# Moving the normalisation of the linear heads one slot earlier in a hybrid decoder block

## The chip, the cores and the metric

The kernel runs on one core of one Trainium2 chip. Its time is the device time in microseconds of one launch. The engines are TensorE (PE, with its weight loads as PEld), VectorE (DVE), ScalarE (ACT), GpSimd (POOL) and SyncE (SP, which here issues nearly all transfers).

## What is computed

A decoder block: a combined input projection of the normalised input, four linear-recurrence heads and eight attention heads over a window of 128 tokens, an output projection, a gated feed-forward network and a last normalisation. The change touches what follows the recurrence of the linear heads, and the norm of the next tokens' input:

```python
def rmsnorm(x, g):
    xf = x.astype(jnp.float32)
    y = xf * lax.rsqrt(jnp.mean(xf * xf, axis=-1, keepdims=True) + EPS)
    return (y * g.astype(jnp.float32)).astype(x.dtype)
...
    o = o_intra + jnp.einsum('bhnck,bhnkv->bhncv', q_dec, s_prev)
    o = o.transpose(0, 2, 3, 1, 4).reshape(bsz, s, A_HEADS, A_DV)
    o = o * lax.rsqrt(jnp.mean(o * o, axis=-1, keepdims=True) + EPS)
    o = o.reshape(bsz, s, A_WIDTH) * norm_g.astype(f32) * jax.nn.silu(g.astype(f32))
...
        u = rmsnorm(h, ln1_g[l])
        proj = u @ w_in[l]
```

There are 2048 tokens, the model is 1024 wide, a linear head has 128 keys and 128 values, and everything is float32.

## The kernel before

The tokens come in four blocks of 512 (`it`, 0 to 3). Every engine has its own program, written out by hand, and waits for the others at semaphores. For each block the mixers run in 27 **slots** (0 to 26), then `out_b` does the last four columns of the output projection. After the four blocks come the feed-forward products, in two pairs of blocks. A product of float32 operands is made of three matmuls of split halves (lines 850 to 852): high by high, low by high, high by low. The halves of a weight tile are made by ACT (`make_hi`, L1217) and DVE (`make_lo`, L1685).

In slots 0 to 21 PE first does one group of 24 such matmuls (a column of the input projection), then small pieces of the mixers. In slots 22 to 26 the groups are those of the output projection by `A_PLAN`: input parts 0 and 1 in slot 22, 2 in slot 23, 4 and 5 in slot 24, 6 in slot 25, 7 and 3 in slot 26; part 3 is the last linear head.

The linear head `a` begins in slot `F_SLOT[a]` (4, 9, 14, 18), and its steps have offsets from there. Before the change the output is made at offset 5 (slots 9, 14, 19, 23), the root and the factor at 6 (slots 10, 15, 20, 24), the turn and the gate at 7 (slots 11, 16, 21, 25). The steps of one head, in order:

- PE `output` (L1015, L1021), and ACT squares and sums it per token block (L1277, `output`), both in the slot of OUTPUT.
- ACT `head_sum` takes the root (L1283, `hnrm`). Root on the one side, and exponential and tanh on the other, need different function tables in ACT, so a table load stands before each change of kind. DVE `head_sum` takes the reciprocal (L1814) and multiplies (L1816, `sqo`). In head 0 the root of the block before for the second norm goes with it (L1358, L1998). These are the steps of NORM_SUM.
- PE `head_turn` transposes `sqo` (L1029) after the group of its slot; DVE `head_mul` multiplies by the gate (L1827); ACT splits off the high half (L1289), DVE `head_lo` the low half (L1832). These are the steps of NORM_MUL.

In the slot loop of DVE `head_sum` stands near the end and `head_mul` near the start, ahead of `make_lo`:

```python
                    mul = head_at(slot, NORM_MUL)
                    if mul is not None:
                        head_mul(it, mul)
                    n = unit_made_at(slot)
                    if n is not None:
                        wait_unit_used(dve, it, n)
                        make_lo(it, n)
```

Around these steps, at the end of a block:

- Slot 21 has the sum of the attention squares on PE (L866), which waits for POOL's addition (L2321, semaphore `s_oacc`); POOL gets to it after the keys of head 3 (L2271, L2274), which wait for DVE's second reciprocal of slot 20 (L1774).
- Slot 21 also has PE's turn of head 3's values (L978) and ACT's copy of it (`iv`, L1262). PE waits for that copy at `key_turn` (L999) in slot 22, after 12 matmuls.
- Slots 19 to 26 have `x_turn` (L1041 on PE, L1328 on ACT): eight transposes that bring the input tokens into the bank that the residual is made from. The first four read first halves, the last four, in slots 23 to 26, second halves, into the same buffers `xs`. SP issues the second halves (L573) in `mixers`, in its one queue: behind the weights of unit 25 the first, of unit 26 the second, of unit 27 the third, of unit 28 the fourth. The weights of unit 27 (L562) wait until DVE has made the low half of unit 25, since both use one buffer. In the last block all four second halves are issued ahead of unit 26.
- ACT makes the sums of squares of the next block's first two token blocks (`stats`, L1224) and their root (`roots`, L1230) in slot 21, DVE scales by them in slot 24 (L1698). In the last block the first splits of the feed-forward operands (L1503 on ACT, L2013 on DVE) stand there, and their loads (L632) in SP's queue behind those of units 26 to 28.

Of the kernel before, what the change touches and what calls it, by code (L numbers as in the profile page):

```python
# [67 lines left out]
BV_TURN = 3  # L68
SWA_SUM, SWA_MUL = 21, 22

KEY_PRODUCTS, V_TURN, KEYS, UPDATE, OUTPUT, NORM_SUM, NORM_MUL = 2, 3, 3, 4, 5, 6, 7

H_TURN, H_STORE, H_SPREAD, H_SCALE = 2, 6, 11, 12
X_LOAD, X_STATS, X_SCALE = 12, 21, 24
# [22 lines left out]
def unit_made_at(slot):  # L97

    return {23: None, 24: 25, 25: 26, 26: None}.get(slot, slot + 2)
# [14 lines left out]
def head_part(slot):  # L114

    for a, first in enumerate(F_SLOT):
        if 0 <= slot - first < 4:
            return a, slot - first
    return None, None


def head_at(slot, offset):

    return F_SLOT.index(slot - offset) if slot - offset in F_SLOT else None
# [7 lines left out]
def block_program(nc, x, ln1_g, w_in, lb_logits, hgrn_norm_g, attn_sinks, attn_norm_g, w_out, ln2_g,  # L132
# [3 lines left out]
    NSB = S // T  # L136
# [33 lines left out]
    with ExitStack() as ctx:  # L170
# [90 lines left out]
        def tile(name, k, shape=(P, T), dt=F32):  # L261
            return at(name, shape, mix_at + 2 * K * k, dt)
# [8 lines left out]
        pr_dump = tile("pr_dump", 12, (P, D))  # L271
# [12 lines left out]
        x_next = [os_[0], os_[1], xs[0], xs[1]]  # L284
# [230 lines left out]
        def wait_unit_used(eng, it, n):  # L515

            eng.wait_ge(s_group, it * UNITS + n - 1)
# [690 lines left out]
        def _(act):  # L1208
# [4 lines left out]
            def make_hi(it, n):  # L1213

                s, k = n % 2, it * UH + n // 2
                act.wait_ge(s_raw[s], k * 16 + 16)
                A(whi[s][:, :, :], raw[s][:, :, :], ACT.Copy).then_inc(s_hi[s], 1)  # L1217


            def stats(it, b, src, dump):  # L1220
                act.wait_ge(s_x0[b], it * 16 + 16)
                if b:
                    act.wait_ge(s_xss, it * TB + b)
                A(dump[:, :], src[:, :], ACT.Square, accum_out=xss[:, b:b + 1]).then_inc(s_xss, 1)  # L1224

            def roots(it, b0, b1):
                act.wait_ge(s_xss, it * TB + b1)
                if it:
                    act.wait_ge(s_xn, it * TB)
                A(xnrm[:, b0:b1], xss[:, b0:b1], ACT.Sqrt, scale=1.0 / D, bias=epst[:, 0:1]).then_inc(s_xroot, 1)  # L1230
# [9 lines left out]
            def head_group(it, a, part, bank):  # L1240
                if part == 0:
                    if a:
                        act.wait_ge(s_ktr, it * HEADS + a)
                    A(forget[:, :], bank, ACT.Tanh, scale=0.5).then_inc(s_tf, 1)
                if part == 1:
                    if a:
                        act.wait_ge(s_qdec, it * HEADS + a)
                    A(gateq[:, :], bank, ACT.Tanh, scale=0.5).then_inc(s_tq, 1)
                if part == 2:
                    if a:  # L1250
                        act.wait_ge(s_ivtr, it * HEADS + a)
                    A(ivT[:, :], bank, ACT.Copy).then_inc(s_iv, 1)
                if part == 3:
                    if a >= 2:
                        act.wait_ge(s_yalo, it * HEADS + a - 1)
                    A(gate[a % 2][:, :], bank, ACT.Tanh, scale=0.5).then_inc(s_tg, 1)
# [7 lines left out]
            def key_turn(it, a):  # L1264
                act.wait_ge(s_ktr, it * HEADS + a + 1)
                if a:
                    act.wait_ge(s_upd, it * HEADS + a)
                A(kst[:, :, :], X[3][:, :].rearrange("p (b k) -> p b k", b=TB), ACT.Copy).then_inc(s_kz, 1)
# [18 lines left out]
            def head_mul(it, a):  # L1287
                act.wait_ge(s_ya, it * HEADS + a + 1)
                A(yhi[:, a, :], gate[a % 2][:, :], ACT.Copy).then_inc(s_yahi, 1)  # L1289
# [33 lines left out]
            def x_turn(it, j):  # L1323
                half, b = divmod(j, TB)
                act.wait_ge(s_xtr, it * 2 * TB + j + 1)
                if it and b == 0:
                    act.wait_ge(s_ust, 32 * (it - 1) + 16 * half + 16)
                A(h_main[:, 4 * half:4 * half + 4, b * P:(b + 1) * P],  # L1328
                  X[0][:, :].rearrange("p (c t) -> p c t", c=4), ACT.Copy).then_inc(s_xT, 1)
# [46 lines left out]
            def slots(it):  # L1376
                for slot in range(SLOTS):
                    a = head_at(slot, UPDATE)
                    if a is not None:
                        key_turn(it, a)  # L1380
                    n = unit_made_at(slot)
                    if n is not None:
                        wait_unit_used(act, it, n)
                        make_hi(it, n)
                    bank = M[slot % 3][:, :]
                    if slot < IN_GROUPS:
                        act.wait_ge(s_group, it * UNITS + slot + 1)
                    if slot == V_SLOT:
                        A(ivT[:, :], bank, ACT.Copy).then_inc(s_bvT, 1)
                    if slot == BV_TURN:  # L1390
                        act.wait_ge(s_vtr, it + 1)
                        act.wait_ge(s_vcar, it + 1)
                        A(vals[:, 1:TB + 1, :], X[1][:, :].rearrange("p (b k) -> p b k", b=TB),
                          ACT.Copy).then_inc(s_vals, 1)
                    if slot == K_SLOT:
                        act.wait_ge(s_kcar, it + 1)
                        for g in range(KV):
                            rows = slice(64 * g, 64 * g + 64)
                            for half in (rows, slice(64 - 64 * g, 128 - 64 * g)):
                                A(kk[half, 0, g, BLOCK:BLOCK + T], bank[rows, :], ACT.Copy).then_inc(s_khi, 1)  # L1400
                    if slot in Q_SLOT:
                        p = Q_SLOT.index(slot)
                        if p >= 2:
                            act.wait_ge(s_score, it * STEPS + (p - 1) * TB)
                        for par in range(2):
                            rows = slice(64 * par, 64 * par + 64)
                            last = A(qs[p % 2][par][rows, :], bank[rows, :], ACT.Copy)
                        last.then_inc(s_qhi, 1)
                    a, part = head_part(slot)
                    if a is not None:  # L1410
                        head_group(it, a, part, bank)
                    a = head_at(slot, NORM_MUL)
                    if a is not None:
                        head_mul(it, a)
                    if slot == X_STATS and it + 1 < NSB:
                        for b in range(2):
                            stats(it + 1, b, x_next[b], pr_dump)
                        roots(it + 1, 0, 2)
                    if slot == SWA_SUM:
                        act.wait_ge(s_ssum, it + 1)  # L1420
                        A(snrm[:, :], X[1][:, 0:TB], ACT.Sqrt, scale=1.0 / (PAIRS * P),
                          bias=epst[:, 0:1]).then_inc(s_sroot, 1)
                    if slot == SWA_MUL:
                        swa_hi(it, 0)
                    for begin, step in ((P_TURN, p_turn), (SCORE, scores), (PV, pv)):
                        i = step_at(slot, begin)
                        if step is scores and it and 0 <= slot - H_TURN - 1 < TB:
                            h_square(it - 1, slot - H_TURN - 1)
                        if i is not None:
                            step(it, i)  # L1430
                    for offset, step in ((V_TURN, iv_turn), (OUTPUT, output), (NORM_SUM, head_sum)):
                        a = head_at(slot, offset)
                        if a is not None:
                            step(it, a)
                    if it and 0 <= slot - H_TURN < TB:
                        h_turn(it - 1, slot - H_TURN)
                    if it and slot == H_SPREAD:
                        h_factor(it - 1)
                    if slot == X_SCALE and it + 1 == NSB:
                        op_hi(0, B11)  # L1440
                    if slot == X_SCALE + 1 and it + 1 == NSB:
                        op_hi(0, B21)
                    if 0 <= slot - XT_SLOT < 2 * TB:
                        x_turn(it, slot - XT_SLOT)
                    if slot == SWA_MUL:
                        for p in range(1, PAIRS):
                            swa_hi(it, p)
# [923 lines left out]
```

## Time and profile before

| | us |
|---|---|
| median of 3 timed runs | 2237.4 |
| the three runs | 2236.55 to 2240.46 |
| the profiled execution, its own time | 2238.9 |
| its span in the trace | 2236.8 |
| PE busy | 2182.2 (98%) |
| DVE busy | 1440.9 (64%) |
| ACT busy | 1011.2 (45%) |
| POOL busy | 442.4 (20%) |

The trace has one row per instruction or run of like instructions: its start, its length, its engine and line, what it writes and reads. In brackets stands how long the engine was idle before it and what ended that. No bracket means that the engine wasn't idle for longer than a tenth of a microsecond. Matmuls overlap, so the distance from one start to the next is their cost, not the length of one.

### The profile page before, as it was taken

Reading aid. Unit: us, or ns where it says so; the run is one execution under the profiler, and the core shown is the slowest. Engines: PE = TensorE matmul, PEld = TensorE weight load, DVE = VectorE, ACT = ScalarE, POOL = GpSimd, SP = SyncE. Lnnn points to the kernel's source line nnn. Section 1 sums busy time; section 2 is a strip of 40 time slices with the busy share of each in tenths; the row PEclk is TensorE's granted clock in tenths of the full one; section 3 lists DMA queues with packets and bytes.
Section 4 is the critical chain, followed back from the end, with each engine's and each line's share of the span. In section 5 each row is a group of like instructions: output and inputs, shape, how many; then the busy total and the mean of one; then the engine's idle time right before and its main releaser. Section 6 shows DMA issues by size and latency. Waiting matters only on the chain.

```text
span 2236.8 us, 29696 instructions
## 1 busy us (share of the span) xinstructions
PE 2182.2 (98%) x10952; PEld 1806.8 (81%) x10952; DVE 1440.9 (64%) x2170; ACT 1011.2 (45%) x1829; POOL 442.4 (20%) x344
## 2 busy tenths in 40 slices
PE   7999999999999999999999999999999999999997
PEld 6887887888878887878888887888888888887886
DVE  5776578657766677765667675568665646554555
ACT  5554455536553555544433333346533333333444
POOL 1231023201220122042233331000322222210000
PEclk9999999999999999999999999999999999999999
DMA  4222333233233313533355655787442323326766
GB/s 123 85 86 74 116 114 99 90 110 126 69 116 109 113 58 123 198 110 112 135 185 202 232 196 195 260 269 260 164 141 90 122 90 109 104 88 228 230 207 216
DMA packets 260704, 321.78 MB, mean 144 GB/s; under 512 B 17233, under 2 KB 168785, under 8 KB 259537
## 3 DMA queue, kind: packets, MB, share of 16 engines
q1 hardware_dynamic: 259984, 317.79, 43.1%
q8 instruction: 88, 1.44, 0.3%
q10 hardware_dynamic: 576, 2.10, 0.2%
q14 instruction: 56, 0.45, 0.1%
HBM read 242.76 MB, written 77.07 MB: 143 GB/s over the span
## 4 chain that ended last, share of the span: by engine, by line
PE 89%; DVE 5%; issue 2%; ACT 2%; DMA 2%; SPq 0%; POOL 0%; DVEq 0%; ACTq 0%; POOLq 0%
PE M L1154 9%; PE M L1156 9%; PE M L1155 9%; PE M L850 7%; PE M L852 7%; PE M L851 7%; PE M L1181 3%; PE M L1182 3%; PE M L1183 3%; PE X L1183 3%; PE X L1182 3%; PE X L1181 3%; PE X L1156 3%; PE X L1155 3%; PE X L1154 3%
## 5 line engine op out<-in xcount | busy, mean ns | idle before, releaser
L2138 DVE TENSOR_TENSOR ring_lo<-ring_raw,ring_hi 128x1024 fp32r<-128x1024 f32 x154 | 189.9, 1233 | 170.4 <-ACT ring_hi L1588 170.0
L1685 DVE TENSOR_TENSOR wlo<-raw,whi 128x1024 fp32r<-128x1024 f32 x120 | 156.0, 1300 | 213.1 <-ACT whi L1217 212.9
L850 PE MATMUL M<-uhi,whi 128*128 128x512 f32 (+1 forms) x720 | 286.0, 397 | 3.7 <-DVE wlo L1685 2.1
L852 PE MATMUL M<-uhi,wlo 128*128 128x512 f32 (+1 forms) x720 | 278.8, 387 | 0.0
L851 PE MATMUL M<-ulo,whi 128*128 128x512 f32 (+1 forms) x720 | 278.3, 386 | 0.0
L1588 ACT ACTIVATE ring_hi<-ring_raw 128x1024 fp32r<-128x1024 f32 x154 | 163.4, 1061 | 234.7 <-DMA ring_raw<-a_scr 231.4
L1154 PE MATMUL M<-t_hi,wu_hi 128*128 128x512 f32 x616 | 240.8, 391 | 4.1 <-DVE gq L2054 2.3
L1156 PE MATMUL M<-t_hi,wu_lo 128*128 128x512 f32 x616 | 240.7, 391 | 0.0
L1155 PE MATMUL M<-t_lo,wu_hi 128*128 128x512 f32 x616 | 240.3, 390 | 0.0
L1217 ACT ACTIVATE whi<-raw 128x1024 fp32r<-128x1024 f32 x120 | 126.7, 1056 | 197.0 <-PE M L852 146.2
L2022 DVE TENSOR_TENSOR wu_lo<-fraw,wu_hi 128x512 fp32r<-128x512 f32 x132 | 127.7, 976 | 120.1 <-ACT wu_hi L1529 119.7
L2282 POOL TENSOR_TENSOR pr<-pr,rd 128x512 f32<-128x512 f32 x64 | 82.6, 1291 | 530.4 <-DVE rd L1718 530.4
L850 PEld LDWEIGHTS M<-uhi,whi 128*128 128x128 f32 x720 | 136.4, 189 | 34.7 <-issue 6.5
L852 PEld LDWEIGHTS M<-uhi,wlo 128*128 128x128 f32 x720 | 136.4, 189 | 27.9
L2334 POOL TENSOR_TENSOR fs<-fraw 128x512 f32<-128x512 f32 x44 | 63.7, 1447 | 476.5 <-DMA fraw<-in_w_gate_dram 209.8
L851 PEld LDWEIGHTS M<-ulo,whi 128*128 128x128 f32 x720 | 136.6, 190 | 24.4
L1154 PEld LDWEIGHTS M<-t_hi,wu_hi 128*128 128x128 f32 x616 | 115.9, 188 | 29.6 <-DVE wu_lo L2022 5.6
L1155 PEld LDWEIGHTS M<-t_lo,wu_hi 128*128 128x128 f32 x616 | 116.1, 188 | 24.2
L1156 PEld LDWEIGHTS M<-t_hi,wu_lo 128*128 128x128 f32 x616 | 115.9, 188 | 24.1
L2340 POOL TENSOR_TENSOR fraw<-fraw,fs 128x512 f32<-128x512 f32 x44 | 58.6, 1331 | 361.6 <-DVE wl_lo L2022 361.6
L1298 ACT ACTIVATE pr<-pr,nm 128x256 f32<-128x256 f32 x128 | 64.1, 502 | 138.0 <-DVE nms L1744 138.0
L1181 PE MATMUL M<-ring_hi 128*128 128x512 f32 x308 | 120.4, 391 | 5.8 <-DVE ring_lo L2138 5.8
(280 smaller groups left out, 5034.3 us busy)
## 6 DMA issues: line engine op xcount, KB each, us to landing
raw<-in_w_in_dram SPq DMA_DIRECT2D x88, 512.0 KB, 3.8
ring_raw<-a_scr SPq DMA_DIRECT2D x154, 256.0 KB, 3.6
fraw<-in_w_gate_dram SPq DMA_DIRECT2D x44, 512.0 KB, 4.5
fraw<-in_w_up_dram SPq DMA_DIRECT2D x44, 512.0 KB, 4.8
a_scr<-au SPq DMA_DIRECT2D x88, 256.0 KB, 2.4
ring_raw<-t_scr SPq DMA_DIRECT2D x88, 256.0 KB, 3.0
ring_raw<-in_w_down_dram SPq DMA_DIRECT2D x66, 256.0 KB, 3.0
raw<-in_w_out_dram SPq DMA_DIRECT2D x32, 512.0 KB, 4.0
```

Of the source, the lines that this page charges most:

```text
L850: mm(bank, whi[s][:, kb, :], hi, start=first, stop=False)
L851: mm(bank, whi[s][:, kb, :], lo, start=False, stop=False)
L852: return mm(bank, wlo[s][:, kb, :], hi, start=False, stop=last)
L1154: mm(bank[:, :], wh[:, k, :], hi[:, k, :], start=start and k == 0, stop=False, skip_group_check=True)
L1155: mm(bank[:, :], wh[:, k, :], lo[:, k, :], start=False, stop=False, skip_group_check=True)
L1156: last = mm(bank[:, :], wl[:, k, :], hi[:, k, :], start=False, stop=k == KH - 1, skip_group_check=True)
L1181: mm(banks[b][:, :], hi[:, 1, tokens], hi[:, 0, :], start=first, stop=False, skip_group_check=True)
L1182: mm(banks[b][:, :], hi[:, 1, tokens], lo[:, 0, :], start=False, stop=False, skip_group_check=True)
L1183: done = mm(banks[b][:, :], lo[:, 1, tokens], hi[:, 0, :], start=False, stop=last, skip_group_check=True)
L1588: A(hi[:, :, :], raw_r[:, :, :], ACT.Copy).then_inc(s_rowhi, 1)
L1685: V.tensor_tensor(wlo[s][:, :, :], raw[s][:, :, :], whi[s][:, :, :].bitcast(F32), ALU.subtract).then_inc(s_lo[s], 1)
L2138: V.tensor_tensor(lo[:, :, :], raw_r[:, :, :], hi[:, :, :].bitcast(F32), ALU.subtract).then_inc(s_rowlo, 1)
```

## The change

Two offsets become smaller by one: root, factor and multiplication move into the slot of the squares (9, 14, 19, 23), and turn and gate follow in slots 10, 15, 20, 24. `stats` of the next block's first two token blocks leaves ACT's slot 21: the first goes to the end of slot 19, the second to the end of slot 20. `roots` stays in slot 21.

```diff
-KEY_PRODUCTS, V_TURN, KEYS, UPDATE, OUTPUT, NORM_SUM, NORM_MUL = 2, 3, 3, 4, 5, 6, 7
+KEY_PRODUCTS, V_TURN, KEYS, UPDATE, OUTPUT, NORM_SUM, NORM_MUL = 2, 3, 3, 4, 5, 5, 6
...
                     if slot == X_STATS and it + 1 < NSB:
-                        for b in range(2):
-                            stats(it + 1, b, x_next[b], pr_dump)
                         roots(it + 1, 0, 2)
...
                     if 0 <= slot - XT_SLOT < 2 * TB:
                         x_turn(it, slot - XT_SLOT)
+                    if X_STATS - 2 <= slot < X_STATS and it + 1 < NSB:
+                        b = slot - X_STATS + 2
+                        stats(it + 1, b, x_next[b], pr_dump)
```

On PE only `head_turn` moves. This is the piece for head 0, in slots 10 and 11 of the first block (`whi` and `wlo` are the weights' halves, `kk` and `qs` the attention keys and queries):

```order
 L851 MATMUL M<-ulo,whi_55 128x512
 L852 MATMUL M<-uhi,wlo_57 128x512
+L1029 MATMUL X<-ident,sqo 128x128 x4
 L942 MATMUL X<-kk,qs_117 128x256 x2
 L942 MATMUL X<-kk,qs_118 128x256 x2
...
 L851 MATMUL M<-ulo,whi_56 128x512
 L852 MATMUL M<-uhi,wlo_58 128x512
-L1029 MATMUL X<-ident,sqo 128x128 x4
 L942 MATMUL X<-kk,qs_117 128x256 x2
 L942 MATMUL X<-kk,qs_118 128x256 x2
```

The transpose stands one group of 24 matmuls earlier, still right behind a group.

On DVE, slots 23 to 25 of the second block, before. The names are `sqo`, the normalised head; `os`, the next block's tokens; `wlo_58` the low half of unit 25, and the `wlo_57` behind it that of unit 26:

```order
L1842 TENSOR_TENSOR ylo<-oT_124,yhi 128x512
L1685 TENSOR_TENSOR wlo_58<-raw_54,whi_56 128x1024
L1814 RECIPROCAL hrnrm<-hnrm 128x4
L1816 TENSOR_TENSOR sqo<-X,hrnrm 128x512
L1693 RECIPROCAL xrn<-xnrm 128x2
L1698 SCALAR_TENSOR_TENSOR os_69<-os_69,xrn,g1row 128x1024
L1698 SCALAR_TENSOR_TENSOR os_70<-os_70,xrn,g1row 128x1024
L1827 SCALAR_TENSOR_TENSOR gate_115<-X,ga,gate_115 128x512
L1685 TENSOR_TENSOR wlo_57<-raw_53,whi_55 128x1024
L1832 TENSOR_TENSOR ylo<-gate_115,yhi 128x512
```

And after, where the line numbers from here on are higher by one:

```order
L1843 TENSOR_TENSOR ylo<-oT_124,yhi 128x512
L1815 RECIPROCAL hrnrm<-hnrm 128x4
L1817 TENSOR_TENSOR sqo<-X,hrnrm 128x512
L1828 SCALAR_TENSOR_TENSOR gate_115<-X,ga,gate_115 128x512
L1686 TENSOR_TENSOR wlo_58<-raw_54,whi_56 128x1024
L1833 TENSOR_TENSOR ylo<-gate_115,yhi 128x512
L1694 RECIPROCAL xrn<-xnrm 128x2
L1699 SCALAR_TENSOR_TENSOR os_69<-os_69,xrn,g1row 128x1024
L1699 SCALAR_TENSOR_TENSOR os_70<-os_70,xrn,g1row 128x1024
L1686 TENSOR_TENSOR wlo_57<-raw_53,whi_55 128x1024
```

The gate's product, which reads what PE turned, stood behind the low half of unit 25 and stands ahead of it now.

On ACT, slots 19 to 21 of the second block, before (`h` is the copy of `x_turn`, `pr_dump` the target of `stats`):

```order
L1277 ACTIVATE sqo,oss<-X 128x128 x4
L1328 ACTIVATE h<-X 128x4x128
L1217 ACTIVATE whi_55<-raw_53 128x1024
L1252 ACTIVATE ivT<-M 128x512
L1317 ACTIVATE gu_64<-oT_124 128x512
L1283 ACT_TABLE_LOAD
L1283 ACTIVATE hnrm<-oss,epst 128x4
L1328 ACTIVATE h<-X 128x4x128
L1217 ACTIVATE whi_56<-raw_54 128x1024
L1256 ACT_TABLE_LOAD
L1256 ACTIVATE gate_115<-M 128x512
```

And after:

```order
L1277 ACTIVATE sqo,oss<-X 128x128 x4
L1283 ACT_TABLE_LOAD
L1283 ACTIVATE hnrm<-oss,epst 128x4
L1328 ACTIVATE h<-X 128x4x128
L1224 ACTIVATE pr_dump,xss<-os_69 128x1024
L1217 ACTIVATE whi_55<-raw_53 128x1024
L1252 ACTIVATE ivT<-M 128x512
L1289 ACTIVATE yhi<-gate_114 128x512
L1317 ACTIVATE gu_64<-oT_124 128x512
L1328 ACTIVATE h<-X 128x4x128
L1224 ACTIVATE pr_dump,xss<-os_70 128x1024
```

The root with its table load went from behind `gu` to right behind the squares, and one sum of the input's squares closes each of the two slots. POOL's and SP's instructions are in the same order as before.

## Rows read from the trace of the kernel before

**Rows 1.** Waits of PE, 100 to 950 us: total, times, longest.

```profile
PE X L1029 <- DVE sqo L1816: 11.7, 12, 1.2
PE X L1041 <- DMA xs<-in_x_dram: 3.0, 4, 1.0
PE X L999 <- ACT iv L1262: 2.9, 2, 1.5
```

**Rows 2.** Timeline of ACT and PE, slots 9 to 11, second block: start, length, [idle<-ended by].

```profile
329.78 0.21 ACT L1277 ACTIVATION_READ_ACCUMULATOR sqo<-X 128x1 f32 x1
...
337.79 1.28 ACT L1283 ACT_TABLE_LOAD   x1
...
332.18 0.65 PE L942 MATMUL X<-kk,qs 128*128 128x256 f32 x4
...
340.37 0.66 PE L1029 MATMUL X<-ident,sqo 128*128 128x128 f32 x4 [0.84 <-DVE sqo L1816]
```

**Rows 3.** The same, slots 14 and 15: first block, then second.

```profile
138.83 0.20 ACT L1277 ACTIVATION_READ_ACCUMULATOR sqo<-X 128x1 f32 x1
...
141.59 0.29 PE L942 MATMUL X<-kk,qs 128*128 128x256 f32 x1
...
373.18 0.21 ACT L1277 ACTIVATION_READ_ACCUMULATOR sqo<-X 128x1 f32 x1
...
375.47 0.41 PE L942 MATMUL X<-kk,qs 128*128 128x256 f32 x2
```

**Rows 4.** Timeline of POOL and PE, slot 21, second block.

```profile
424.07 1.27 POOL L2321 TENSOR_TENSOR gu<-gu,gu 128x512 f32<-128x512 f32 x1
...
425.35 0.66 PE L1029 MATMUL X<-ident,sqo 128*128 128x128 f32 x4 [1.25 <-DVE sqo L1816]
425.84 0.95 PE L866 MATMUL X<-ones,gu 128*128 128x1 f32 x8
```

**Rows 5.** Timeline of ACT and PE, slots 21 and 22, second block.

```profile
428.11 1.05 ACT L1224 ACTIVATE pr_dump<-os 128x1024 f32<-128x1024 f32 x1
...
432.15 0.59 ACT L1262 ACTIVATE iv<-X 128x512 f32<-128x512 f32 x1
...
432.88 0.63 PE L999 MATMUL X<-ident,forget 128*128 128x128 f32 x4
```

**Rows 6.** Timeline of DVE and SP, slots 24 and 25, second block.

```profile
448.68 1.22 DVE L1685 TENSOR_TENSOR wlo<-raw,whi 128x1024 fp32r<-128x1024 f32 x1 [1.09 <-ACT whi L1217]
...
453.89 0.75 DVE L1827 SCALAR_TENSOR_TENSOR gate<-X,ga,gate 128x512 f32<-128x512 f32 x1 [0.58 <-PE X L1029]
454.61 1.23 DVE L1685 TENSOR_TENSOR wlo<-raw,whi 128x1024 fp32r<-128x1024 f32 x1
...
450.34 0.58 SPq L573 DMA_DIRECT2D xs<-in_x_dram  x1
```

**Rows 7.** Timeline of PE, slots 24 to 26, second block.

```profile
450.04 0.60 PE L1041 MATMUL X<-ident,xs 128*128 128x128 f32 x4
...
453.25 0.60 PE L1029 MATMUL X<-ident,sqo 128*128 128x128 f32 x4
454.78 0.66 PE L1041 MATMUL X<-ident,xs 128*128 128x128 f32 x4 [0.92 <-DMA xs<-in_x_dram]
...
461.34 0.66 PE L1041 MATMUL X<-ident,xs 128*128 128x128 f32 x4 [0.41 <-DMA xs<-in_x_dram]
```

**Rows 8.** Timeline of ACT and PE, slots 24 and 25, last block.

```profile
915.20 1.90 ACT L1503 ACTIVATE b_hi<-b_raw 128x2048 fp32r<-128x2048 f32 x1
...
916.57 0.60 PE L1041 MATMUL X<-ident,xs 128*128 128x128 f32 x4
...
920.22 0.60 PE L1041 MATMUL X<-ident,xs 128*128 128x128 f32 x4
```

**Rows 9.** Windows: stretch, length, busy by engine, granted clock, DMA share, GB/s.

```profile
427.00:430.00 3.00, 3.00 (x17) 3.00 (x15) 2.12 (x3) 2.90 (x6) 0.00 (x0) 0.50 0.29 90
2026.00:2029.00 3.00, 2.98 (x13) 2.48 (x14) 1.58 (x2) 1.69 (x2) 0.00 (x0) 1.00 0.73 280
```

## The prediction

> **What bounds the kernel now.** The page gives PE 98% of the span, so time moves only where a wait of PE goes or comes. The first view is PE's waits over the four blocks of the mixers [rows 1]; the reader is to see that three kinds touch this change. PE waits 12 times for `sqo` at L1029: once for head 0, once for head 1 (0.84 us each, as at 340.37 in [rows 2]) and once for head 2 (1.25 us, [rows 4]) in each block, 11.7 us in all. It waits twice for ACT's `iv` at L999, 1.5 us each, and four times for `xs` at L1041, 3.0 us in all. The second view is the timeline around these places. Head 3's turn in slot 25 has no wait [rows 7].
>
> **Root and factor, heads 0 and 1.** Nothing is added or removed; the chain load, root, reciprocal, multiplication only starts sooner. From the start of the table load to the start of PE's turn it is 340.37 - 337.79 = 2.58 us [rows 2]. In the new place it follows the squares. For head 0 these end at 329.78 + 0.21 = 329.99, so the turn can start at 332.57. PE has ended its group at 332.18, where L942 starts now [rows 2]: a wait of 0.4 replaces one of 0.84. Gain 0.45 in each of four blocks, 1.8. For head 1 in the second block: 373.39 + 2.58 = 375.97 against 375.47, wait 0.5, gain 0.34; in the first block, where DVE has no second norm to scale, 139.03 + 2.58 = 141.61 against 141.59, wait none, gain 0.8 [rows 3]. With the third and fourth like the second: 0.8 + 3 x 0.34 = 1.8. The second switch, back to tanh, now falls before L1248 of the next slot instead of before an exponential; DVE reads that tanh only after its score steps, some 3 us on, which hides it. DVE, which now waits for the root at the end of its slot, has the denominators of the next slot queued behind; POOL and then PE need these one slot later, so they are cover enough.
>
> Here the trace is to be held against a page. The load takes 1.28 us, and the next instruction follows it within 0.02 [rows 2]. The Trainium skill, page "ScalarE: Activation LUTs", section "What ACT_TABLE_LOAD costs", says that a switch costs a drain of about 1.38 us besides its 1.28, some 2.66 together. The duration agrees; the drain isn't to be seen in this trace, where the load stands right behind an exponential. By that page the chain would be longer in all eight places; what this would give is the third rival.
>
> **Head 2.** The turn moves from slot 21 to slot 20, where its chain is done well before PE's group. What is late next in slot 21 is POOL: PE's sum L866 waits for L2321, which ends at 424.07 + 1.27 = 425.34 [rows 4]. Its chain hangs on a reciprocal of DVE in slot 20, and the gate's product now stands ahead of that; but DVE waits there for ACT's `whi` anyway, so it becomes about 0.1 later: 425.5. L866 started at 425.84. Gain 0.35 and not 1.25, four times: 1.4. PE idles there 0.9 us still. Bounds: none to 1.25.
>
> **Input statistics.** Two sums of about 1.2 us (1.05 and a read, [rows 5]) and a split leave ACT's slot 21; the second sum now ends about 0.8 after ACT would have begun slot 21. So `iv` comes some 2.2 us sooner: 432.15 becomes 429.9, done at 430.5. PE, which reached L999 at 432.88 [rows 5], will be there at about 431.1, so no wait is left. The wait is 1.47 in the first and third blocks (2.9 in 2, [rows 1]). In the second block PE doesn't wait because its granted clock is 0.50 there, the lower of its two levels (1.2 GHz), after it had idled for 1.25 us and done thin work [rows 4, 9]; that fall took the same 1.5 us from it. I count 3 x 1.47 = 4.4. The last block has no statistics and no such wait. At the ends of slots 19 and 20 ACT idles until PE's next group is done, which hides the first sum and all but 0.8 of the second.
>
> Gains so far: 1.8 + 1.8 + 1.4 + 4.4 = 9.4.
>
> **Head 3, where the cost is.** In slot 24 PE's turn stands behind two parts of the output projection, at 450.04, where the `x_turn` of slot 24 is now [rows 7]. DVE's gate product waits for it and stands ahead of the low half of unit 25, which DVE makes in the middle of that slot, at 448.68 [rows 6]. By today's spacing the product starts 453.89 - 453.25 = 0.64 after the turn [rows 6, 7], and the low half 454.61 - 453.89 = 0.72 after the product [rows 6]: 450.04 + 0.64 + 0.72 = 451.40, that is 2.72 late. PE doesn't need that half before slot 26. But SP does: the weights of unit 27 wait for it, and the third second half of the tokens is queued behind them. It is issued at 450.34 and PE can read it at 454.78, 4.44 later, having waited 0.92 [rows 6, 7]. Now: issued at 453.06, read at 457.50. PE is ready no later than before, so it idles 3.6 us, and everything behind is 2.72 late. The fourth half waited 0.41 in the second block [rows 7] and has cover now. Three blocks: 3 x 2.72 - 0.41 = 7.8. The four waits of today are 0.4 to 1.0 [rows 1, 7], so landings vary by some 0.5, and each block's cost lies between 2.2 and 3.3.
>
> In the last block all four second halves are issued earlier, so this path doesn't exist. There ACT waits for the gate before it splits its high half and then the first feed-forward operand (1.90 us, [rows 8]); its copy for `x_turn` is behind both. The turn takes the place at 916.57 [rows 8], the product runs from 0.64 to 1.39 after it (0.75 long, [rows 6]), then 0.6 for the high half (a copy of 512 columns, as `iv` in [rows 5]), 1.90, and 0.6 for the copy: 921.1 against PE's 920.22, cost 0.8. The operand loads also start 2.7 later behind unit 27, and DVE's combinations with them; the low half of unit 28 comes then about 0.5 after PE wants it. Sum 1.3, bounds 0 to 3.5.
>
> **The clock.** Three waits of 3.6 us in front of dense work are longer than any in the mixers before. What this does is uncertain. The clock fell after 1.25 us of idle in the second block and didn't after the same wait in three others, nor after one of 2.5 at 2026 [rows 9]. A fall costs 1.5. Bounds: no falls, 0; one at each long wait, 4.5. I take two of three, 3.0, as these waits exceed both examples.
>
> The Trainium skill, page "TensorE: Matmul & The Clock Gate", section "HAM oscillation — how this bites in real kernels", says that a wait for a transfer can throttle the array every time it repeats. By that all three waits would cost, 4.5 in all and 1.5 more than the sum takes. Only the fall at 427 bears it out so far; the wait at 2026 speaks against a fall at every wait.
>
> **Sum.** -9.4 + 7.8 + 1.3 + 3.0 = +2.7. Against the profiled execution's own 2238.9 (span 2236.8 and 2.1 around it) that is 2241.6; that execution is 1.5 above the median of the three, so the median becomes 2237.4 + 2.7 = 2240.1.
>
> **Rivals.**
> First, the half isn't late: the transfer lands sooner, or DVE's wait in slot 24 is short. For it: the tokens' halves are only 256 KB. Against: the order on DVE is fixed and SP waits in order. Then 2237.4 - 9.4 + 1.3 = 2229.3, clearly faster. Chance 0.12.
> Second, slower: the clock. Each long wait makes it fall, and so do the 0.9 us of idle with the thin L866 in slot 21 in two blocks of four: 5 falls, 7.5. Then 2237.4 - 9.4 + 9.1 + 7.5 = 2244.6. For it: the fall at 427 came at that place. Against: that wait gets shorter by 0.3. It decides from four falls on. Chance 0.2.
> Third, a switch of tables costs twice its load when it stands behind the squares: 1.28 more in eight chains, 10.2, so 2250.3. Against: no idle time around the load now [rows 2]. Chance 0.03.
> That the gains don't come because DVE's longer slots 10 and 15 delay PE elsewhere: DVE takes the gate's product and the low half there instead of one slot later, 0.9 us more, and its results of a slot are read a slot later. It would be worth the 3.6 of heads 0 and 1, 2243.7; chance 0.05, within the second's time.
>
> **How the numbers follow.** A measurement of this kernel can tell about 0.2% from no change, 4.5 us: faster is below 2232.9, slower above 2241.9. The forecast has 0.6 (its own range 2236.5 to 2242.5, from no falls to three and the bounds of the last block). Faster is the first rival, 0.13 with a little from outside. Slower is the second, third and fourth and a small part of the forecast's own range: 0.30. The rest is 0.57. The range that leaves out the first and third rival runs from 2233 to 2245.
>
> **What would show it.** In the trace after: L1029 with waits of 0.4 to 0.5 in slots 10 and 15, none in slots 20 and 24; L866 waiting 0.9 for POOL; L999 without a wait; DVE's product ahead of the low half in slot 24 with an idle of about 2 us before it; L1041 in slot 25 waiting 3.6 us for `xs` in three blocks and 0.8 for ACT in the last. Wrong would be an L1041 that waits 1 us as before, or waits of PE at L954 or L942, which have none now.

## The result: 0.2% slower

The changed kernel takes 2241.7 us (median of 15 runs, 2238.1 to 2246.8) against 2237.4 (15 runs, 2235.7 to 2240.6). The ratio is 1.0021, 95% interval 1.0013 to 1.0028: slower by 4.3 us, where 2.7 were forecast. The interval leaves out 1, so with 15 runs each these 4.3 us can be told from no change; the forecast had put that limit at 4.5. The profiled execution took 2242.9 with a span of 2240.8.

The page of the changed kernel, busy time by engine, differs by little:

```profile
PE 2185.0 (98%) x10952; PEld 1807.5 (81%) x10952; DVE 1438.3 (64%) x2170; ACT 1011.1 (45%) x1829; POOL 444.6 (20%) x344
```

PE's waits between 100 and 950 us are other ones than before [rows 1]:

```profile
PE X L1041 <- DMA xs<-in_x_dram: 11.5, 3, 4.5
PE X L866 <- POOL gu L2322: 4.3, 4, 1.1
PE X L1029 <- DVE sqo L1817: 1.8, 6, 0.4
PE X L1015 <- DVE st L1805: 1.5, 4, 0.4
PE X L1041 <- ACT h L1328: 0.7, 1, 0.7
```

Before, 11.7 us stood at L1029, 3.0 at L1041 and 2.9 at L999. Of L1029's 11.7 there are 2.1 left (head 0's turn in the first block, 0.25 us at 98.25, lies just ahead of this window), and the last is gone: 12.5 us. In their place are 4.3 for POOL, 8.5 more for `xs` and 0.7 for ACT: 13.5. All that was freed is given back in waits, and 1 us more.

The turn in slot 10 of the second block, and where PE would have gone on (the matmul before starts at 332.16 and costs 0.23):

```profile
330.22 1.28 ACT L1283 ACT_TABLE_LOAD   x1
...
332.16 0.39 PE L852 MATMUL M<-uhi,wlo 128*128 128x512 f32 x1
332.81 0.44 PE L1029 MATMUL X<-ident,sqo 128*128 128x128 f32 x2 [0.26 <-DVE sqo L1817]
```

From the load to the turn it is 2.59 us, against 2.58 in [rows 2]. The turn starts 0.42 after PE could have gone on; the 0.26 in brackets is less because idle time is counted from the end of the last matmul, which overlaps the next start. Slot 21 now waits for POOL, as the timelines of POOL and PE show:

```profile
423.48 1.27 POOL L2322 TENSOR_TENSOR gu<-gu,gu 128x512 f32<-128x512 f32 x1
...
424.81 1.05 PE L866 MATMUL X<-ones,gu 128*128 128x1 f32 x8 [1.08 <-POOL gu L2322]
...
430.35 0.60 PE L999 MATMUL X<-ident,forget 128*128 128x128 f32 x4
```

And this is the place that decides, slots 24 and 25, on PE, DVE, SP and PE again:

```profile
447.50 0.49 PE L1029 MATMUL X<-ident,sqo 128*128 128x128 f32 x3
...
448.13 0.75 DVE L1828 SCALAR_TENSOR_TENSOR gate<-X,ga,gate 128x512 f32<-128x512 f32 x1 [2.28 <-PE X L1029]
448.80 1.22 DVE L1686 TENSOR_TENSOR wlo<-raw,whi 128x1024 fp32r<-128x1024 f32 x1
...
450.04 0.37 SPq L562 DMA_DIRECT2D raw<-in_w_out_dram  x1
450.45 0.58 SPq L573 DMA_DIRECT2D xs<-in_x_dram  x1
...
454.67 0.59 PE L1041 MATMUL X<-ident,xs 128*128 128x128 f32 x2 [3.40 <-DMA xs<-in_x_dram]
```

DVE idles 2.28 us for the turn, the product and the low half follow, then SP is released, and PE idles 3.40 us. The chain is 447.50 + 0.63 + 0.67 = 448.80 for the low half; the forecast's spacing was 0.64 and 0.72. The low half began at 448.68 before too, but PE is ahead by now: it does at 447.50 what stood at 450.04 [rows 7]. Against PE the low half is 448.80 - (448.68 - 2.54) = 2.66 us late, where 2.72 were forecast.

Behind each of the three long waits the granted clock is at its lower level, 1.2 GHz. The kernel before has one such fall in the four blocks of the mixers, in slot 21 of the second [rows 9]; the changed kernel has these three and none in slot 21. Windows; the third figure from the end of a row is the clock, in parts of 2.4 GHz:

```profile
219.50:222.50 3.00, 2.71 (x9) 2.33 (x10) 0.00 (x0) 0.60 (x1) 0.00 (x0) 0.50 0.95 300
455.00:458.00 3.00, 3.00 (x10) 2.47 (x9) 0.00 (x0) 0.60 (x1) 0.00 (x0) 0.50 0.87 255
690.50:693.50 3.00, 3.00 (x9) 2.42 (x8) 0.00 (x0) 0.60 (x1) 0.00 (x0) 0.50 0.92 284
```

### The profile page after: what moved, and what is told of

It reads as the page before. It is cut to its first block, busy times and chain, and to the rows that moved or that the text cites. A ratio compares the mean times of both kernels' runs of the same rounds, so it can differ in the third digit from the quotient of the medians.

```text
span 2240.8 us, 29696 instructions
## 1 busy us (share of the span) xinstructions
PE 2185.0 (98%) x10952; PEld 1807.5 (81%) x10952; DVE 1438.3 (64%) x2170; ACT 1011.1 (45%) x1829; POOL 444.6 (20%) x344
## 4 chain that ended last, share of the span: by engine, by line
PE 84%; DVE 7%; issue 2%; DMA 2%; ACT 2%; POOL 1%; SPq 1%; DVEq 0%; POOLq 0%; ACTq 0%
PE M L1154 9%; PE M L1156 9%; PE M L1155 9%; PE M L850 7%; PE M L852 7%; PE M L851 7%; PE M L1181 3%; PE M L1182 3%; PE M L1183 3%; PE X L1181 3%; PE X L1183 3%; PE X L1182 3%; PE X L1156 3%; PE X L1154 3%; PE X L1155 3%
## 5 line engine op out<-in xcount | busy, mean ns | idle before, releaser
L1154 PE MATMUL M<-t_hi,wu_hi 128*128 128x512 f32 x616 | 241.0, 391 | 4.4 <-DVE gq L2055 2.6
L1154 PEld LDWEIGHTS M<-t_hi,wu_hi 128*128 128x128 f32 x616 | 115.9, 188 | 29.9 <-DVE wu_lo L2023 5.9
```

What stands on the lines that cost most here:

```text
L1154: mm(bank[:, :], wh[:, k, :], hi[:, k, :], start=start and k == 0, stop=False, skip_group_check=True)
```

## The experiments

The theory: heads 0 to 2 gain as forecast, the moved gate of head 3 puts its wait in front of a low half, SP's queue carries it to the tokens' second halves, and the idle brings the clock down. The ratios are to the kernel before, in runs of the same chip and hour.

### The gate behind the low half

One edit of the changed kernel, on DVE:

```diff
-                    if mul is not None:
+                    if mul is not None and mul < HEADS - 1:
                         head_mul(it, mul)
                     n = unit_made_at(slot)
                     if n is not None:
                         wait_unit_used(dve, it, n)
                         make_lo(it, n)
+                    if mul == HEADS - 1:
+                        head_mul(it, mul)
```

> The changed kernel, but on DVE head 3's gate product stands behind the low half of unit 25 in slot 24, as before the change; all else is as changed. Theory A (the product's wait delays that low half, SP's queue with the tokens' second halves stands behind it, and the clock falls at the long waits): the low half comes in the middle of slot 24 again, the third second half of the tokens is issued about 2.7 us sooner, the 11.5 us of PE's waits for xs in three blocks become about 3 to 5 (0.9 at the third half and up to 1 at the fourth, since the low half of unit 26 now follows the scaling of the next tokens), the clock falls there go with them (3 x 1.7), and the median is 2228 to 2232. Theory B (the transfers are slow in that place for another reason, such as other traffic): L1041 keeps waits of 3.4 us or more and the median stays at 2240 to 2243.

Measured: 2231.6 us, ratio 0.9969 (0.9959 to 0.9980). PE's waits for `xs`:

```profile
PE X L1041 <- DMA xs<-in_x_dram: 4.8, 6, 1.1
```

All as theory A had it: 0.7 to 1.1 us at the third half and 0.6 to 0.8 at the fourth. That the waits at the fourth come from the low half of unit 26, which now follows the scaling, wasn't tested. The order of two instructions on DVE is worth the whole loss and more.

### The halves first in SP's queue

DVE stays as changed; SP issues sooner:

```diff
                     if it + 1 < NSB:
-                        load_half(it, 1, c - 4)
+                        for b in {4: (0,), 5: (1, 2, 3)}.get(c, ()):
+                            load_half(it, 1, b)
```

> The changed kernel with DVE's order as changed, but SP issues all but the first of the tokens' second halves ahead of the weights of unit 27, as in the last block. Theory A (it is the place in SP's queue that makes the delay of the low half cost PE time): DVE still makes the low half of unit 25 late, but L1041 waits for xs nowhere in slots 25 and 26, no clock fall is left there, and the median is 2224 to 2228. Theory B (DVE's late low half costs PE time itself, by unit 25 or the units behind it): waits of 2 us or more appear at the matmuls of slot 26 or of out_b, and the median stays above 2236.

Measured: 2231.8 us, ratio 0.9968 (0.9955 to 0.9980). L1041 (L1042 here) waits for no transfer any more, though DVE's low half starts 1.30 us after the turn (446.27), as in the changed kernel:

```profile
446.91 0.75 DVE L1829 SCALAR_TENSOR_TENSOR gate<-X,ga,gate 128x512 f32<-128x512 f32 x1 [2.27 <-PE X L1030]
447.57 1.22 DVE L1687 TENSOR_TENSOR wlo<-raw,whi 128x1024 fp32r<-128x1024 f32 x1
```

So a late low half costs PE nothing by itself; it is the queue behind it. The median is some 4 us above what theory A gave. The timed runs have a mean clock of 0.995 to 0.996, no better than those of the changed kernel. The profiled one, the slowest of the five, has three falls in the mixers, all in slot 21 behind L866's wait for POOL, instead of in slot 25. That was not expected, and it is what the last three experiments are about.

### Only the root sooner

The changed kernel, its moved statistics too, with turn and gate left at offset 7:

```diff
-KEY_PRODUCTS, V_TURN, KEYS, UPDATE, OUTPUT, NORM_SUM, NORM_MUL = 2, 3, 3, 4, 5, 5, 6
+KEY_PRODUCTS, V_TURN, KEYS, UPDATE, OUTPUT, NORM_SUM, NORM_MUL = 2, 3, 3, 4, 5, 5, 7
```

> Root, factor and multiplication a slot sooner as in the change, statistics moved as in the change, but turn and gate left in their old slots 11, 16, 21 and 25. Theory A (all 11.7 us of waits at the turn were waits for the product, and the costs of the change came with the moved gate alone): no wait at L1029 is left, a wait of about 0.7 for POOL stands at L866 in slot 21 four times, L999 has no wait, L1041 waits 3 us in all as before, and the median is 13 us below that of the kernel before, 2223 to 2227. Theory B (the sooner root costs elsewhere, by DVE's wait for it at the end of the slot): waits appear at the scores or at their transposes, and the median is 2230 or more.

Measured: 2222.7 us, ratio 0.9936 (0.9923 to 0.9948). PE's waits from 80 to 950 us:

```profile
PE X L1041 <- DMA xs<-in_x_dram: 4.2, 4, 1.4
PE X L866 <- POOL gu L2322: 3.5, 4, 0.9
PE X L1015 <- DVE st L1805: 1.5, 4, 0.4
PE M L1154 <- DVE wu_lo L2023: 0.9, 1, 0.9
```

Theory A in the main: no wait is left at L1029 or L999. L866 waits 0.9 and not 0.7, and L1041 4.2 in all and not 3; the median is 14 us below the kernel before by the ratio, 13 were expected. The wait at L1154 belongs to the feed-forward products and fell behind 950 us before. So root and statistics alone are worth 0.6%, and the third step, one slot for turn and gate, costs 0.85%.

### The statistics apart

Back in slot 21 in the changed kernel:

```diff
                     if slot == X_STATS and it + 1 < NSB:
+                        for b in range(2):
+                            stats(it + 1, b, x_next[b], pr_dump)
                         roots(it + 1, 0, 2)
...
-                    if X_STATS - 2 <= slot < X_STATS and it + 1 < NSB:
-                        b = slot - X_STATS + 2
-                        stats(it + 1, b, x_next[b], pr_dump)
```

> The changed kernel with both sums of the input's squares back in ACT's slot 21; the offsets of the heads are as changed. Theory A (the 1.5 us waits at L999 went because of the moved statistics): the waits return in three blocks, 1.2 to 1.5 us each, and the median is 3.5 to 4.5 above the changed kernel's. Theory B (they went mostly because root and high half of head 2 left slots 20 and 21 of ACT): by the lengths in the trace iv then comes 0.3 to 0.6 us after PE wants it, so L999 waits about 1.5 us in all and the median is 1 to 2 above the changed kernel's.

Measured: 2247.9 us, ratio 1.0051 (1.0036 to 1.0066), 6 to 7 above the changed kernel, more than either theory gave. In the profiled execution there is one wait at L999:

```profile
PE X L999 <- ACT iv L1262: 0.9, 1, 0.9
```

In the other two blocks the clock has fallen in slot 21 and there is no wait at L999, as in the second block of the kernel before. It falls at the three long waits too, once for twice as long:

```profile
191.50:194.00 2.50, 2.50 (x14) 2.50 (x13) 0.69 (x1) 2.41 (x4) 0.00 (x0) 0.50 0.60 160
222.00:225.00 3.00, 3.00 (x10) 2.51 (x10) 0.00 (x0) 0.60 (x1) 0.00 (x0) 0.50 0.80 245
458.00:463.00 5.00, 4.90 (x14) 4.03 (x15) 0.00 (x0) 0.60 (x1) 0.00 (x0) 0.50 0.80 256
```

The mean clock of the four timed runs is 0.991 to 0.994, against 0.993 to 0.997 of the changed kernel's. The wait of 0.9 lies midway between theory B's 0.3 to 0.6 and A's 1.2 to 1.5, so it decides for neither. Between 80 and 950 us all of PE's waits together are 20.1 us, as in the changed kernel, so the 6 us aren't waiting. The profiled execution took 9.6 us longer than the changed kernel's. In it the clock falls five times in the mixers, once for twice as long, against three times there, and two more times in the feed-forward products. That accounts for most of it. Why it falls so much more often here isn't shown.

The other way round, the kernel before with the statistics alone moved:

```diff
-KEY_PRODUCTS, V_TURN, KEYS, UPDATE, OUTPUT, NORM_SUM, NORM_MUL = 2, 3, 3, 4, 5, 5, 6
+KEY_PRODUCTS, V_TURN, KEYS, UPDATE, OUTPUT, NORM_SUM, NORM_MUL = 2, 3, 3, 4, 5, 6, 7
```

(the diff is against the changed kernel).

> The kernel before with only the sums of the input's squares moved to the ends of ACT's slots 19 and 20; the heads' offsets are as before. Theory A (the moved statistics are what frees L999): no wait at L999, 3 us less of waits, median 2 to 4 below the kernel before. Theory B (the second sum stands in front of slot 21's high half and gate, so half of what it frees it delays): waits of about 0.5 at L999 in three blocks, the waits at L1029 unchanged at 0.8, 0.8 and 1.2, and the median 1 to 3 below the kernel before.

Measured: 2236.6 us, ratio 0.9996 (0.9986 to 1.0006), no difference that these runs can tell. The waits:

```profile
PE X L1029 <- DVE sqo L1817: 11.7, 12, 1.2
PE X L1041 <- DMA xs<-in_x_dram: 3.9, 5, 1.0
...
PE X L999 <- ACT iv L1262: 0.6, 3, 0.2
```

Of 2.9 us at L999, 0.6 are left, 0.2 in each of three blocks; 0.9 more stand at L1041, as would follow if PE reaches the transfer sooner. The moved statistics do free most of L999, theory B's 0.5 a block was too much. Of PE's waits 1.4 us are gone in these blocks; the time moved by something between 3 us less and 1 us more.

### The clock

First the long wait was filled in the changed kernel. PE does 13 matmuls of 512 columns more, into an unused bank:

```diff
                 half, b = divmod(j, TB)
+                if j == 6 and it + 1 < NSB:
+                    pe.wait_ge(s_yb, it * PAIRS + PAIRS)
+                    for _ in range(13):
+                        mm(X[1][:, :], yhi[:, 0, 0:P], yhi[:, 1, :], start=True, stop=True)
                 pe.wait_ge(s_xh[b], it * 32 + 16 * half + 16)
```

> The changed kernel with 13 matmuls of 512 columns more on PE in slot 25 of the first three blocks, ahead of the third second half's transpose; they write an unused bank and their result isn't read, so they only fill about 3 us of the wait of 3.4 to 4.5. Theory A (the clock falls because PE idles there, and each of the three falls costs 1.7): the transposes start when they did, the clock stays at its upper level behind them, and the median falls by 4 to 5 us to 2236 to 2238. Theory B (the falls cost nothing, since PE is bound by something else after them, or have another cause): the median stays within 1.5 us of the changed kernel's.

Measured: 2241.9 us, ratio 1.0021 (1.0011 to 1.0030): no gain at all, against theory A. The number is theory B's, but not its reason, that falls cost nothing. The windows behind the wait in slot 25 and behind L866 in slot 21 tell why; the first is slot 25 of the first block, the others slot 21 of the second, third and fourth:

```profile
219.50:222.50 3.00, 3.00 (x15) 2.45 (x14) 0.00 (x0) 0.45 (x1) 0.00 (x0) 1.00 0.87 273
424.50:427.50 3.00, 3.00 (x13) 2.71 (x12) 1.43 (x3) 2.66 (x5) 0.00 (x0) 0.50 0.80 255
660.00:663.00 3.00, 3.00 (x11) 2.55 (x10) 1.06 (x3) 2.30 (x5) 0.00 (x0) 0.50 0.81 261
895.50:898.50 3.00, 3.00 (x10) 2.52 (x9) 0.77 (x2) 1.78 (x4) 0.00 (x0) 0.50 0.88 301
```

The clock holds where the filling is, at 1.00 in all three blocks, and falls at the other thin place, where it didn't in the changed kernel's profile: three falls here, three there. So the two places were taken one after the other. First, slot 21 cleared: the sum L866 stands behind the other small products.

```diff
-                    if slot == SWA_SUM:
-                        pe.wait_ge(s_oacc, it * (PAIRS - 1) + PAIRS - 1)
-                        sums(X[1], sqs[0], s_ssum)
                     if slot == SWA_MUL:
                         pe.wait_ge(s_srr, it + 1)
...
+                    if slot == SWA_SUM:
+                        pe.wait_ge(s_oacc, it * (PAIRS - 1) + PAIRS - 1)
+                        sums(X[1], sqs[0], s_ssum)
                     if it and slot == H_SPREAD:
                         h_spread(it - 1)
```

> The changed kernel with one edit: on PE the sum L866 stands behind the score products and the value turn in slot 21. Theory A (falls of the clock come at any place with enough idle or thin work; slot 21 is one of two such places): L866 has no wait, no fall comes in slot 21, those at the three waits for xs stay, and the median is 4 to 6 below the changed kernel's: 4.3 for the waits and up to 2 for falls, 2236 to 2238. Theory B (the waits for POOL only move into the long waits for xs): L1041 waits 1 us longer in each block and the median stays above 2240.

Measured: 2240.3 us, ratio 1.0008 (0.9999 to 1.0017). The waits are as theory A had them, none at L866 and no more at L1041; the time isn't. By the ratios some 3 us come and not 4 to 6, with intervals that overlap, and the median is above theory B's 2240.

```profile
PE X L1041 <- DMA xs<-in_x_dram: 10.8, 3, 3.6
PE X L1029 <- DVE sqo L1817: 2.1, 7, 0.4
```

The mean clock of the runs is 0.992 to 0.995, lower than with the wait in slot 21. Then the same with the filling:

> The same with 13 filling matmuls ahead of the third second half's transpose in slot 25 of three blocks. Theory A (with slot 21 out of the way the falls at the long waits are the only ones left in the mixers, and each costs 1.7): no fall in the mixers, and the median is 4 to 5 below the same kernel without the filling, 2231.5 to 2233.5. Theory B (a fall costs less than half of its length, or filling moves it elsewhere again): the median is less than 2 below the same kernel without the filling.

Measured: 2234.1 us, ratio 0.9979 (0.9968 to 0.9989), 6.2 us less than without the filling, more than theory A's 4 to 5. The transposes of slot 25 start no sooner by it, at 218.74 and 451.34 in the first two blocks against 218.45 and 451.13. The clock holds in all three blocks, and in the timed runs it is 0.996 to 0.998:

```profile
218.00:223.00 5.00, 4.55 (x23) 3.61 (x22) 0.42 (x1) 0.60 (x1) 0.00 (x0) 1.00 0.65 217
451.00:456.00 5.00, 4.66 (x23) 3.91 (x24) 0.00 (x0) 0.60 (x1) 0.00 (x0) 1.00 0.74 249
684.00:689.00 5.00, 4.85 (x23) 4.07 (x24) 0.00 (x0) 0.60 (x1) 0.00 (x0) 1.00 0.77 258
```

What one fall costs can be read from the two profiles. From the transposes of slot 25 in the first block to those in the second it is 232.7 us without and 232.6 with the filling, and neither has a fall there. From the second to the third it is 234.3 and 232.8, and only the first has a fall: 1.4 us. The profiled execution without the filling has one fall and one of twice the length, and none behind the first of its three long waits:

```profile
218.50:221.50 3.00, 3.00 (x16) 2.52 (x16) 0.00 (x0) 0.60 (x1) 0.00 (x0) 1.00 0.80 243
```

It is the fastest of its eleven runs, only 2.6 us above the profiled one with the filling. In the timed runs the time follows the clock: 2236.7 to 2239.4 us at 0.995, 2243.3 to 2245.2 at 0.992. So the 6.2 us between the medians go with the clock, but how many falls the median run has isn't known. The runs also lie closer together, 2231.8 to 2235.1 against 2236.7 to 2245.2.

### Put together

The root sooner, turn and gate in their old slots, the statistics moved, and the halves first in SP's queue (the edits shown above):

> Root, factor and multiplication sooner, turn and gate in their old slots, statistics moved, and SP issues the tokens' second halves ahead of the weights of unit 27. Theory A (the waits of 0.8 to 1.4 us for xs, 4.2 in all with only the root moved, come from the place in SP's queue): L1041 has no wait, and the median is 3.5 to 5 below that with only the root moved, 2217.5 to 2219.5. Theory B (the halves compete with other transfers, or the weights behind them then come late): a wait for weights appears in out_b, and the median stays within 2 of the one with only the root moved.

Measured: 2219.2 us, ratio 0.9918 (0.9903 to 0.9933), 0.18% better than with only the root sooner. That is theory A, no wait is left at L1041 (L1042 here), though the two intervals overlap. And with L866 behind the other small products of slot 21:

> The same as the one with the root sooner and the halves first, and on PE the sum of the attention squares L866 stands behind head 3's score products and value turn in slot 21. Theory A (its wait of 0.9 us for POOL is the next one, and PE has other work for that time; the clock falls behind it in some executions): no wait in slot 21, no fall there, and the median is 3.5 to 6 lower than without this edit, 2212 to 2216. Theory B (ACT's root of the sum and iv come later by it, so L999 or the spread behind it waits): waits of about 1 us at L999 or L857 and no change of the median by more than 1.

Measured: 2215.1 us, ratio 0.9898 (0.9883 to 0.9913), 1.0% below the kernel before, theory A again; its slowest run is below the fastest of the one before it. Its waits from 80 to 930 us are one line (the first long waits of the feed-forward products, 2.7 and 0.9 us for DVE, stand right behind):

```profile
PE X L1016 <- DVE st L1806: 1.4, 4, 0.3
```

## Why the prediction was right, and where its sizes were off

The direction, the mechanism and the time were right (2240.1 forecast, 2241.7 measured). Step by step:

- Heads 0 and 1: waits of 0.4 and 0.5 forecast by starts, and none for head 1 in the first block. Measured 0.25 and 0.34 to 0.37 by idle time, which is 0.42 by starts for head 0; none in that block. The forecast took a distance of starts (0.4) from an idle time (0.84); in idle time alone heads 0 and 1 gain 4.6 in four blocks and not 3.6. The drain that the Trainium skill's page "ScalarE: Activation LUTs" adds in "What ACT_TABLE_LOAD costs" isn't seen here either: the root starts 1.30 us after the load's start.
- Head 2: POOL late next by 0.9, measured 1.08. The gain is 0.7 in four blocks and not 1.4.
- L999: no wait, as forecast; PE is there at 430.35 and `iv` was begun at 428.54. The forecast named two sums and a split that leave slot 21. The experiments agree that both count: the statistics moved alone leave 0.2 a block, and put back in the changed kernel they bring back 0.9, not the whole 1.5, in the block without a fallen clock. How the two share it isn't settled. 1.5 of its 4.4 us were not a wait but the fall in the second block, so they belong to the clock.
- Head 3: 3.6 us of idle in three blocks forecast, 4.47, 3.40 and 3.63 measured, 11.5 in all; the cause is proved from both ends, by the order on DVE and by the queue on SP. The last block's wait for ACT was 0.7 (0.8 forecast). The low half of unit 28 came in time; instead three waits of the first feed-forward products grew or came, by 1.1 in all, and later ones shrank by 0.6.
- The clock was the term that was too small. All waits of PE in the two profiles add up to 42.7 us before and 44.1 after: 1.4 more, where the forecast's terms without the clock give -7.9 + 7.8 + 1.3 = +1.2. The spans differ by 4.0, which leaves 2.6 for the clock: three falls instead of one. The forecast had two instead of one, 3.0 - 1.5 = +1.5. So the sizes of the waits met almost exactly in sum, by errors of both signs, and one fall more makes most of what is missing.
- The forecast also took a fall as a matter of one wait. It isn't: in two experiments it moved between slot 21 and slot 25. The second rival named this mechanism and both places; its five falls were more than the profile has.

The Trainium skill's page "TensorE: Matmul & The Clock Gate", section "HAM oscillation — how this bites in real kernels", had it that each repeated wait for a transfer costs a fall. The changed kernel's profile agrees, 0.50 behind all three; with the sum last in slot 21 it doesn't hold, for the clock stayed at 1.00 behind the first, a wait of 3.62 us. The fall of before at 427, which the forecast counted for the page, stood behind a wait for DVE and not for a transfer.

That the time moved so little is no sign that little happened. The changed kernel frees 12.5 us of waits and takes on 13.5, and only a list of waits by releaser shows that.

## What to carry to other kernels

When a step is moved up, look at what stands behind it in its engine's program, and follow that to the queues that wait for it: here a gate product was in front of a weight's low half, that in front of a weight load, that in front of the tokens. Two of the three steps moved could go without the third; try a move in parts. Idle time of the matmul engine had a second price here, in the clock, and taking one wait away moved that price to the next thin place. So clear such places together, and judge by the spread of the runs too.

## What was not expected of the hardware

- A fall of the granted clock isn't tied to its longest wait: with waits of 3.4 us or more filled by matmuls it fell in slot 21, after 1.08 us of idle and a product of one column, in three blocks; with that place cleared it fell at two of the three long waits and not at the first, once staying down from before 685 to after 690 us:

```profile
685.00:690.00 5.00, 4.62 (x13) 3.85 (x14) 0.00 (x0) 0.60 (x1) 0.00 (x0) 0.50 0.75 247
```

- Matmuls whose result nobody reads were worth 0.3% (2240.3 to 2234.1 us) by keeping the clock up, once slot 21 was cleared; without that they were worth nothing (2241.7 and 2241.9 us).
- The same wait for the same kind of transfer was 3.40, 3.63 and 4.47 us in one execution. It was issued 2.95 to 2.96 us after the start of the turn in each block; from issue to PE's reading it took 4.22, 4.45 and 5.28.
